# Three orders changed in a two-layer decoder trunk: half 1's first product, the turn of keys and probabilities, VectorE's work in the gating layer

## The chip, the core and the metric

One core of a Trainium2 chip runs the whole program. The metric is device microseconds of one execution, the median of several runs. The engines named here are TensorE (PE; its weight loads are shown apart as PEld), VectorE (DVE), ScalarE (ACT), GpSimd (POOL) and SyncE (SP), which issues nearly all loads. Work on different engines is ordered by semaphores alone.

## The reference

x is (1, 256, 1024) in float32. Two layers follow each other, each of four sub-layers:

```python
def reference(x, p, ...):
    for i in range(DEPTH):                      # DEPTH = 2
        x = layer_norm(DN_ALPHA * x + 0.5 * swiglu(x, w_gate, w_up, w_down), ...)
        m = mixer_attention(x, ...) if i % 2 == 0 else mixer_sgu(x, ...)
        x = layer_norm(DN_ALPHA * x + m, ...)
        x = layer_norm(DN_ALPHA * x + 0.5 * swiglu(x, ...), ...)
        x = x + jax.nn.sigmoid(x @ ple_w_gate[i]) * (p[i] @ ple_w_proj[i])

def mixer_sgu(x, w_in, b_in, ln_g, ln_b, w_s, b_s, w_out):
    u, v = jnp.split(jax.nn.gelu(x @ w_in + b_in), 2, axis=-1)
    v = layer_norm(v, ln_g, ln_b).reshape(...)
    mixed = jnp.einsum('gts,bcsgd->bctgd', jnp.where(causal, w_s, 0), v) + b_s...
    return (u * mixed) @ w_out
```

mixer_attention projects x to queries, keys and values of two groups of 8 heads (head size 64), runs softmax attention with a relative bias in the first group and with a forgetting term in the second, and projects the result back. The feed-forward width is 2816.

## The kernel before

The 256 tokens are two halves of 128, h = 0 and 1. Eight phases follow each other (`PHASES`): feed-forward, attention, feed-forward, gated embedding, and the same with the gating layer (`sgu`) in place of attention.

**Products in two parts.** Each float32 operand is split into a high part (ScalarE's copy into fp32r) and a low part (VectorE's subtraction, L1118). A product is high x high, high x low and low x high, three matmuls for each block of 128 input channels (L388, L389, L390). The stationary operand is the transposed x (xT_hi, xT_lo), the moving one the weights (g_hi, g_lo), 512 columns at a time. One gate product (`g_product`) is 8 blocks x 3 = 24 matmuls in two parts: part 0 takes blocks 0 to 3, whose weights come through rawA, part 1 blocks 4 to 7, through rawB.

**Weights.** SP loads a half of a chunk (two DMAs of 512 KB) into rawA or rawB, ScalarE copies it to g_hi, VectorE subtracts it to g_lo. g_hi and g_lo have two slots. The load of half n into a raw buffer waits for `split_a` or `split_b`, that is until VectorE has subtracted half n - 1 of that same buffer (`load_half`). A product of half 0 waits for the same semaphores before each of its parts.

**Borders between phases.** x is normalised half by half, turned by TensorE into the tp banks (L466, four 128x128 transposes for each of two blocks j), copied high by ScalarE (signal `tp_hi[j]`) and low by VectorE (signal `tp_taken[j]`). `g_product_turning` makes half 0's first product of a phase and puts half 1's transposes in front of and behind its last block. Half 1's first product follows; `x_wait` makes it wait for `tp_taken`, so for both parts of x, before each of its parts.

**Attention.** The order of the phase is written out in `ATTN_ORDER`, which TensorE, ScalarE and VectorE all walk. `("turn", c, h)` turns projected queries or keys from stage into tp bank h, `("probs", n)` turns head n's probabilities into bank n % 2, `("values", n)` multiplies heads 2n and 2n+1 with the values, and `("g front", 5, 0)` and `("g back", 5, 0)` are the two parts of a gate product. ScalarE's copy of probabilities n into probsT (L830) also waits until the values of head n - 2 are done with probsT. VectorE copies the turned keys to kT (L1383).

**Gating layer.** Eight products (four chunks, two halves) are followed by the output projection, chunks g0+4 and g0+5, in the order of `PAIR`: first chunk half 0, second chunk half 0, first chunk half 1, second chunk half 1. Before them VectorE makes y = gate times u of each half (`gate_y`, L1514, eight instructions), which TensorE turns (`y_turn`) and ScalarE and VectorE split into xT_hi and xT_lo. `biased` (L1505) adds the bias to a product and frees its bank; `lo_g(n, part)` is the subtraction of weight half `part` of chunk n. `y_turn(1)` stands between the two parts of the second of the four products.

Of the kernel before, what the change touches and what calls it, by code (L numbers as in the profile page):

```python
# [62 lines left out]
    ("g", 3, 1), ("probs", 0), ("probs", 1), ("scores", 1), ("exps", 1), ("turn", 3, 0), ("values", 0),  # L63
    ("g", 4, 0), ("probs", 2), ("probs", 3), ("scores", 2), ("exps", 2), ("turn", 3, 1), ("values", 1),
    ("g", 4, 1), ("probs", 4), ("probs", 5), ("scores", 3), ("exps", 3), ("turn", 4, 0),
    ("g front", 5, 0), ("probs", 6), ("probs", 7), ("values", 2), ("turn", 4, 1), ("g back", 5, 0), ("causal", 4),
    ("values", 3), ("scores", 4), ("exps", 4), ("group out", 0), ("causal", 5),
    ("g front", 5, 1), ("probs", 8), ("probs", 9), ("g back", 5, 1), ("scores", 5), ("exps", 5), ("causal", 6),
    ("proj", 0), ("p_copy", 0), ("w_out", 0), ("values", 4), ("w_low", 0), ("proj", 1), ("w_out", 1), ("p_copy", 1),
# [35 lines left out]
def p_use(k, c, h):  # L105


    return 1 if k == P_PHASE and c >= 2 - h else 0
# [24 lines left out]
def build(nc, bucket_onehot, x_in, p_in, ln_g, ln_b, w_gate, w_up, w_down, attn_w_in, attn_b_f, attn_w_out,  # L133
# [15 lines left out]
    with ExitStack() as ctx:  # L149
# [234 lines left out]
        def _(pe):  # L384
# [8 lines left out]
            def g_piece(slot, h, dst, k_from, k_to):  # L393
# [4 lines left out]
                               [g_hi[:, slot, b, :] for b in ks], [g_lo[:, slot, b, :] for b in ks],  # L398
                               first=k_from == 0, last=k_to == KB)

            def g_product(n, slot, h, dst, operand_wait=None, between=None, parts=(0, 1), front=None):
                for part in parts:
                    if operand_wait is not None:
                        operand_wait(part, h)
                    if h == 0:
                        pe.wait_ge((split_a, split_b)[part], n)
                    done = g_piece(slot, h, dst, 4 * part, 4 * part + 4)
                    if part == 0 and front is not None:
                        done.then_inc(front, 1)
                    if part == 0 and between is not None:  # L410
                        between()
                done.then_inc(g_done, 1)
# [101 lines left out]
            for k, (kind, i, s) in enumerate(PHASES):  # L514
# [4 lines left out]
                if kind == "ffn":  # L519
                    def up(c, cs, h, between=None, operand_wait=None):  # L520
                        bank_free(h, u0 + c)
                        g_product(g0 + c, (g0 + cs) % 2, h, gu[h][:, :], operand_wait, between)

                    def turn(c, cs, h):
                        pe.wait_ge(gu_taken[h], u0 + c + 1)
                        transposes(h, t0 + c + p_use(k, cs, h), [stage[:, h, FC + P * b:FC + P * b + P] for b in range(2)])

                    def down(c, cs, h, js=(0, 1)):

                        pe.wait_ge(tp_taken[h], t0 + c + (2 if k == P_PHASE and cs >= 1 else 1))  # L530
                        if k == 0 and cs == 0 and h == 1:
                            pe.wait_ge(bias_sb, 1)
                        at = 2 if h == 1 and cs == NCH - 1 else h
                        d_product(d0 + c, (d0 + cs) % 2, h, hT_hi[:, at], hT_lo[:, at], first=cs == 0,
                                  last=cs == NCH - 1, js=js)

                    def chunk(c, cs):

                        up(c, cs, 0)
                        turn(c - 1, cs - 1, 1)  # L540
                        down(c - 1, cs - 1, 0)
                        up(c, cs, 1)
                        turn(c, cs, 0)
                        down(c - 1, cs - 1, 1)

                    if k == 0:
                        g_first(x_wait)
                    elif PHASES[k - 1][0] == "ple":
                        up(0, 0, 0, half1, x_wait)
                    else:  # L550
                        bank_free(0, u0)
                        g_product_turning(g0, g0 % 2, 0, gu[0][:, :], x_wait, half1_block)
                    if k > 0:
                        up(0, 0, 1, operand_wait=x_wait)
                    if k == 0:
                        pe.wait_ge(bias_in, 32)
                        pe.matmul(acc[1][0:HEADS, 1, :], rel_sb[:, :], onehot_sb, start=True,
                                  stop=True).then_inc(bias_mm, 1)
                    turn(0, 0, 0)
                    chunk(1, 1)  # L560
                    if k == P_PHASE:
                        pe.wait_ge(p_loaded, 16 * (i + 1))
                        for h in range(HALVES):

                            transposes(h, t0 + 2 - h, [p_tok[:, h, P * b:P * b + P] for b in range(2)])
                    with pe.Fori(0, (NCH - 3) // 2) as r:
                        for e in range(2):
                            chunk(r * 2 + (2 + e), 2 + e)


                    c = NCH - 1
                    up(c, c, 0)
                    turn(c - 1, c - 1, 1)
                    down(c - 1, c - 1, 0)
                    turn(c, c, 0)
                    bank_free(1, u0 + c)
                    g_piece((g0 + c) % 2, 1, gu[1][:, :], 0, 2)
                    down(c, c, 0)
                    g_piece((g0 + c) % 2, 1, gu[1][:, :], 2, KB).then_inc(g_done, 1)
                    down(c - 1, c - 1, 1, (0,))  # L580
                    turn(c, c, 1)
                    down(c - 1, c - 1, 1, (1,))
                    use = (t0 + NCH + p_use(k, c, 0), t0 + NCH + p_use(k, c, 1) + 1)
                    ln_turn(0, x0, use)
                    down(c, c, 1)

                    def half1(x0=x0, use=use):
                        ln_turn(1, x0, use)

                    def half1_block(j, x0=x0, use=use):  # L590
                        ln_turn_block(1, j, x0, use)
# [40 lines left out]
                if kind == "attn":  # L632
# [62 lines left out]
                    for e in ATTN_ORDER:  # L695
                        if e[0] == "g":
                            c, h = e[1:]
                            bank_free(h, u0 + c)
                            if c == 0 and h == 0:
                                g_product_turning(g0, g0 % 2, 0, gu[0][:, :], x_wait, half1_block)  # L700
                            else:
                                g_product(g0 + c, (g0 + c) % 2, h, gu[h][:, :], x_wait if c == 0 else None)
                        elif e[0] == "g front":
                            c, h = e[1:]
                            bank_free(h, u0 + c)
# [61 lines left out]
                if kind == "sgu":  # L767
                    def mix(h):

                        pe.wait_ge(vn_ready, 2 * (h + 1))  # L770
                        for g in range(HEADS):
                            done = pe.matmul(acc[h][:, g // 4, P * (g % 4):P * (g % 4) + P], ws_T[:, g, :],
                                             v_sgu[:, h, P * g:P * g + P], start=True, stop=True)
                        done.then_inc(mix_done, 1)

                    def y_turn(h):
                        token_transposes(t_tok, h, t0 + h, [(tok_ready, x0 + 2 * h + j + 1) for j in range(2)])


                    for n, (c, h) in enumerate((c, h) for c in range(4) for h in range(2)):  # L780
                        bank_free(n % 2, u0 + n // 2)
                        if n == 0:
                            g_product_turning(g0 + c, (g0 + c) % 2, h, gu[0][:, :], x_wait, half1_block)
                        else:
                            g_product(g0 + c, (g0 + c) % 2, h, gu[n % 2][:, :], x_wait if c == 0 else None)
                        if n == 0:

                            pe.wait_ge(ws_loaded, 1)
                            for g in range(HEADS):
                                done = pe.transpose(acc[0][:, g // 4, P * (g % 4):P * (g % 4) + P],  # L790
                                                    ws_tok[:, g, :], ident[:, :])
                            done.then_inc(ws_turned, 1)
                        if n == 5:
                            pe.wait_ge(ws_taken, 1)
                            mix(0)
                        if n == 7:
                            y_turn(0)
                            mix(1)
                    use, out0, after = (t0, t0 + 1), g0 + 4, (t0 + 2, t0 + 3)

                    def y_wait(j, h, use=use):
                        pe.wait_ge(tp_taken[j], use[h] + 1)


                if kind in ("attn", "sgu"):
                    for n, (j, h) in enumerate(PAIR):
# [8 lines left out]
                        if n == 3 and kind == "sgu":  # L815
# [2 lines left out]
                                  y_wait if n % 2 == 0 else None, between,  # L818
                                  (1,) if j == 0 and kind == "attn" else (0, 1),
                                  out_front_done if n == 2 and kind == "sgu" else None)  # L820
                    use = after

                    def half1_block(j, x0=x0 + 4, use=use):
                        ln_turn_block(1, j, x0, use)
# [283 lines left out]
        def _(dve):  # L1108
# [19 lines left out]
            def lo_g(n, part):  # L1128
                lo_g_into(n, n % 2, part)
# [103 lines left out]
            for k, (kind, i, s) in enumerate(PHASES):  # L1233
# [264 lines left out]
                if kind == "sgu":  # L1498
# [41 lines left out]
                    biased(6, 3)  # L1540
                    lo_g(g0 + 4, 0)
                    gate_y(0)
                    lo_g(g0 + 4, 1)
                    xT_low(0, v0)
                    biased(7, 3)
                    gate_y(1)
                    for part in range(2):
                        lo_g(g0 + 5, part)
                    residual(0, 0, r0, (g_done, 2 * (g0 + 4) + 1))
                    xT_low(1, v0)  # L1550
                    ln0, out0, end = ln0 + 1, g0 + 4, v0 + 2
# [136 lines left out]
```

## Time and profile before

| | us |
|---|---|
| median of three runs | 1023.72 |
| lowest and highest | 1022.42, 1024.78 |
| the profiled execution | 1023.21 |
| its span | 1021.7 |

| engine | busy us | share of the span |
|---|---|---|
| PE | 1012.8 | 99% |
| PEld | 836.2 | 82% |
| DVE | 610.1 | 60% |
| ACT | 448.5 | 44% |
| POOL | 41.9 | 4% |

The span is the time from the first to the last recorded instruction. A matmul's end is modelled, so TensorE's share says that it is nearly always issued to, not that it runs at its peak. Where a wait matters, the distance between the starts of two instructions is the safer measure.

### The profile page before, as it was taken

What the parts mean: (1) busy time and instruction counts of PE and PEld (TensorE: products, weight loads), DVE (VectorE), ACT (ScalarE), POOL (GpSimd) and SP (SyncE); (2) the same over time, 40 slices, a digit from 0 to 9 for tenths busy, and PEclk for the clock granted to TensorE, in tenths of its full rate; (3) what the DMA queues carried; (4) which work ended last, traced back from release to release, by engine and by line L of the source; (5) the groups of instructions that cost most, each with busy time, mean ns of one, the idle gap of its engine ahead of it and who ended that gap; (6) DMA issues with size and microseconds to landing.
All of it is one profiled execution on the core that took longest, in us unless ns stands there. A gap on an engine that the chain in (4) does not pass through costs nothing.

```text
span 1021.7 us, 12789 instructions
## 1 busy us (share of the span) xinstructions
PE 1012.8 (99%) x4816; PEld 836.2 (82%) x4816; DVE 610.1 (60%) x716; ACT 448.5 (44%) x523; POOL 41.9 (4%) x55
## 2 busy tenths in 40 slices
PE   9999999999999999999999999999999999999998
PEld 7888888888888888888888888888887888888887
DVE  5655455776478745454677544545778864545574
ACT  5444344346473643434356343434344553434441
POOL 0400000100000000000010000000210100000010
PEclk9999999999999999999999999999999999999999
DMA  8875656355236766565539656564467676465531
GB/s 289 283 230 177 208 171 210 114 178 172 83 110 220 250 204 205 164 205 164 165 128 321 210 165 206 165 212 156 135 194 238 204 250 206 164 207 171 196 124 42
DMA packets 129683, 191.47 MB, mean 187 GB/s; under 512 B 5448, under 2 KB 95816, under 8 KB 129520
## 3 DMA queue, kind: packets, MB, share of 16 engines
q1 hardware_dynamic: 126432, 180.11, 53.9%
q0 software_dynamic: 2928, 10.61, 3.1%
q8 instruction: 24, 0.39, 0.2%
q10 hardware_dynamic: 288, 0.26, 0.1%
q14 instruction: 11, 0.09, 0.0%
HBM read 189.90 MB, written 1.06 MB: 187 GB/s over the span
## 4 chain that ended last, share of the span: by engine, by line
PE 93%; DVE 4%; DMA 1%; ACT 1%; issue 1%; SPq 0%; DVEq 0%; ACTq 0%
PE gu L388 19%; PE gu L390 19%; PE gu L389 19%; PE acc L388 10%; PE acc L390 10%; PE acc L389 10%; PE tp L466 4%; DVE g_lo L1118 2%; DMA rawB<-in_sgu_w_in 1%; ACT g_hi L830 1%; PE acc L653 1%; DVE t_tok L1514 0%; DVE xT_lo L1118 0%; DMA x_tok<-in_x 0%; DVE stage L1505 0%
## 5 line engine op out<-in xcount | busy, mean ns | idle before, releaser
L388 PE MATMUL gu<-g_hi,xT_hi 128*128 128x512 f32 x928 | 363.5, 392 | 1.2 <-DVE xT_lo L1118 1.1
L390 PE MATMUL gu<-g_hi,xT_lo 128*128 128x512 f32 x928 | 361.0, 389 | 0.0
L389 PE MATMUL gu<-g_lo,xT_hi 128*128 128x512 f32 x928 | 360.4, 388 | 0.0
L388 PEld LDWEIGHTS gu<-g_hi,xT_hi 128*128 128x128 f32 x928 | 174.3, 188 | 37.5 <-issue 2.4
L390 PEld LDWEIGHTS gu<-g_hi,xT_lo 128*128 128x128 f32 x928 | 174.2, 188 | 36.2
L389 PEld LDWEIGHTS gu<-g_lo,xT_hi 128*128 128x128 f32 x928 | 174.3, 188 | 34.8
L896 ACT ACTIVATE stage<-gu 128x256 f32<-128x256 f32 x88 | 33.7, 383 | 361.2 <-PE gu L390 361.1
L1118 DVE TENSOR_TENSOR g_lo<-rawA,g_hi 128x2048 fp32r<-128x2048 f32 (+2 forms) x66 | 141.5, 2145 | 78.4 <-ACT g_hi L830 78.3
L1118 DVE TENSOR_TENSOR g_lo<-rawB,g_hi 128x2048 fp32r<-128x2048 f32 (+1 forms) x64 | 141.0, 2203 | 18.1 <-ACT g_hi L830 18.1
L1244 DVE SCALAR_TENSOR_TENSOR stage<-stage,gu 128x256 f32<-128x256 f32 x88 | 37.0, 420 | 189.6 <-ACT stage L896 189.6
L388 PE MATMUL acc<-d_hi,hT_hi 128*128 128x512 f32 x352 | 144.8, 411 | 0.0
L830 ACT ACTIVATE g_hi<-rawA 128x2048 fp32r<-128x2048 f32 (+2 forms) x66 | 118.6, 1800 | 46.4 <-DMA rawA<-in_ffn_w_up 26.0
L390 PE MATMUL acc<-d_hi,hT_lo 128*128 128x512 f32 x352 | 138.1, 392 | 0.0
L389 PE MATMUL acc<-d_lo,hT_hi 128*128 128x512 f32 x352 | 137.6, 391 | 0.0
L1118 DVE TENSOR_TENSOR d_lo<-rawD,d_hi 128x2048 fp32r<-128x2048 f32 x45 | 103.1, 2292 | 46.0 <-ACT d_hi L830 46.0
L830 ACT ACTIVATE g_hi<-rawB 128x2048 fp32r<-128x2048 f32 (+1 forms) x64 | 118.3, 1849 | 17.5 <-DMA rawB<-in_ffn_w_up 6.9
L830 ACT ACTIVATE d_hi<-rawD 128x2048 fp32r<-128x2048 f32 x45 | 86.4, 1920 | 6.3 <-DMA rawD<-in_ffn_w_down 4.2
L390 PEld LDWEIGHTS acc<-d_hi,hT_lo 128*128 128x128 f32 x352 | 66.0, 188 | 14.6
L389 PEld LDWEIGHTS acc<-d_lo,hT_hi 128*128 128x128 f32 x352 | 66.5, 189 | 11.6
L388 PEld LDWEIGHTS acc<-d_hi,hT_hi 128*128 128x128 f32 x352 | 66.1, 188 | 11.2
L1626 POOL TENSOR_TENSOR small<-small 128x1 f32<-128x1 f32 x14 | 18.0, 1288 | 879.5 <-DVE small L1155 879.5
L1118 DVE TENSOR_TENSOR hT_lo<-tp,hT_hi 128x256 fp32r<-128x256 f32 x88 | 36.9, 419 | 9.8 <-ACT hT_hi L830 9.8
(181 smaller groups left out, 673.1 us busy)
## 6 DMA issues: line engine op xcount, KB each, us to landing
rawD<-in_ffn_w_down SPq DMA_DIRECT2D x44, 1024.0 KB, 4.9
rawA<-in_ffn_w_gate SPq DMA_DIRECT2D x42, 512.0 KB, 4.0
rawA<-in_ffn_w_up SPq DMA_DIRECT2D x42, 512.0 KB, 4.9
rawB<-in_ffn_w_gate SPq DMA_DIRECT2D x42, 512.0 KB, 4.4
rawB<-in_ffn_w_up SPq DMA_DIRECT2D x42, 512.0 KB, 5.5
rawA<-in_attn_w_in SPq DMA_DIRECT2D x12, 512.0 KB, 4.4
rawB<-in_attn_w_in SPq DMA_DIRECT2D x12, 512.0 KB, 4.9
rawA<-in_ple_w_gate SPq DMA_DIRECT2D x8, 512.0 KB, 4.7
```

Source lines behind the costliest of these rows:

```text
L388: pe.matmul(dst, hi[b], w_hi[b], start=first and b == 0, stop=False)
L389: pe.matmul(dst, hi[b], w_lo[b], start=False, stop=False)
L390: done = pe.matmul(dst, lo[b], w_hi[b], start=False, stop=last and b == len(hi) - 1)
L466: done = pe.transpose(tp[bank][0:src.shape[1], rows * q:rows * q + rows], src, ident[0:rows, 0:rows])
L653: done = pe.matmul(acc[0][:, r, at:at + P], qT[rows, blk, i_q * P:i_q * P + P], kT[rows, blk, keys:keys + P], start=g == 0, stop=g == 0 or ...
L830: return act.activation(dst, src, ACT.Copy, scale=scale)
L896: act.activation(stage[:, h, 0:FC], gu[h][:, 0:FC], ACT.Silu).then_inc(act_done, 1)
L1118: return dve.tensor_tensor(dst, src, hi.bitcast(F32), ALU.subtract)
L1244: dve.scalar_tensor_tensor(out=stage[:, h, FC:2 * FC], in0=stage[:, h, 0:FC], scalar=0.5, in1=gu[h][:, FC:2 * FC], op0=ALU.mult, op1=ALU.m ...
L1626: pool.tensor_tensor(rstd[:, h:h + 1], var_eps[:, h:h + 1], neg_half, ALU.pow)\
```

## The change

Three edits, in one.

1. Half 1's first product of a phase, at the four borders that `g_product_turning` serves, becomes `g_product_high_first`. It waits for `tp_hi[0]` first, makes the eight matmuls of blocks 0 to 3 that take x's high part, then waits for x's low part and makes the four low x high ones. Part 1 is as before.
2. In `ATTN_ORDER` the keys of the second group, half 1, are turned ahead of the values of heads 4 and 5 and of the probabilities of heads 6 and 7.
3. In the gating layer VectorE makes x's low part and the last bias add ahead of weight half B of chunk g0+4, and weight half A of chunk g0+5 ahead of `gate_y(1)`.

```diff
-    ("g front", 5, 0), ("probs", 6), ("probs", 7), ("values", 2), ("turn", 4, 1), ("g back", 5, 0), ("causal", 4),
+    ("g front", 5, 0), ("turn", 4, 1), ("values", 2), ("probs", 6), ("probs", 7), ("g back", 5, 0), ("causal", 4),
...
+            def g_product_high_first(slot, dst, high_use, operand_wait):
+
+                tok = slice(P, 2 * P)
+                pe.wait_ge(tp_hi[0], high_use)
+                for b in range(4):
+                    pe.matmul(dst, xT_hi[:, b, tok], g_hi[:, slot, b, :], start=b == 0, stop=False)
+                    pe.matmul(dst, xT_hi[:, b, tok], g_lo[:, slot, b, :], start=False, stop=False)
+                operand_wait(0, 1)
+                for b in range(4):
+                    pe.matmul(dst, xT_lo[:, b, tok], g_hi[:, slot, b, :], start=False, stop=False)
+                operand_wait(1, 1)
+                g_piece(slot, 1, dst, 4, KB).then_inc(g_done, 1)
...
-                    if k > 0:
+                    if k > 0 and PHASES[k - 1][0] == "ple":
                         up(0, 0, 1, operand_wait=x_wait)
+                    elif k > 0:
+                        bank_free(1, u0)
+                        g_product_high_first(g0 % 2, gu[1][:, :], high_use, x_wait)
...
                     biased(6, 3)
                     lo_g(g0 + 4, 0)
                     gate_y(0)
-                    lo_g(g0 + 4, 1)
                     xT_low(0, v0)
                     biased(7, 3)
+                    lo_g(g0 + 4, 1)
+                    lo_g(g0 + 5, 0)
                     gate_y(1)
-                    for part in range(2):
-                        lo_g(g0 + 5, part)
+                    lo_g(g0 + 5, 1)
                     residual(0, 0, r0, (g_done, 2 * (g0 + 4) + 1))
```

TensorE at the border from the first feed-forward phase to attention, start of half 1's first product; before:

```order
L388 MATMUL gu<-g_hi,xT_hi 128x512 [waits tp_taken0,gu_taken1]
L389 MATMUL gu<-g_lo,xT_hi 128x512
L390 MATMUL gu<-g_hi,xT_lo 128x512
L388 MATMUL gu<-g_hi,xT_hi 128x512
L389 MATMUL gu<-g_lo,xT_hi 128x512
```

and now:

```order
L406 MATMUL gu<-g_hi,xT_hi 128x512 [waits tp_hi0,gu_taken1]
L407 MATMUL gu<-g_lo,xT_hi 128x512
L406 MATMUL gu<-g_hi,xT_hi 128x512
L407 MATMUL gu<-g_lo,xT_hi 128x512
L406 MATMUL gu<-g_hi,xT_hi 128x512
L407 MATMUL gu<-g_lo,xT_hi 128x512
L406 MATMUL gu<-g_hi,xT_hi 128x512
L407 MATMUL gu<-g_lo,xT_hi 128x512
L410 MATMUL gu<-g_hi,xT_lo 128x512 [waits tp_taken0]
L410 MATMUL gu<-g_hi,xT_lo 128x512 x3
L388 MATMUL gu<-g_hi,xT_hi 128x512 [waits tp_taken1]
```

The low-x matmul moved from third place to ninth, and the wait for VectorE's part (tp_taken0) with it.

VectorE in the gating layer, from the gating of half 0 on (t_tok from acc and u_sgu is `gate_y`, stage from gu is `biased`); before:

```order
L1514 SCALAR_TENSOR_TENSOR t_tok<-acc,small,u_sgu 128x128 x7
L1118 TENSOR_TENSOR g_lo<-rawB,g_hi 128x2048 [waits high_b]
L1118 TENSOR_TENSOR xT_lo<-tp,xT_hi 128x4x128 [waits tp_hi0]
L1118 TENSOR_TENSOR xT_lo<-tp,xT_hi 128x4x128 [waits tp_hi1]
L1505 TENSOR_TENSOR stage<-gu,bias_tab 128x512 [waits act_done,g_done]
L1514 SCALAR_TENSOR_TENSOR t_tok<-acc,small,u_sgu 128x128 [waits act_done,mix_done]
L1514 SCALAR_TENSOR_TENSOR t_tok<-acc,small,u_sgu 128x128 x7
L1118 TENSOR_TENSOR g_lo<-rawA,g_hi 128x2048 [waits high_a]
L1118 TENSOR_TENSOR g_lo<-rawB,g_hi 128x2048 [waits high_b]
```

and now:

```order
L1535 SCALAR_TENSOR_TENSOR t_tok<-acc,small,u_sgu 128x128 x7
L1139 TENSOR_TENSOR xT_lo<-tp,xT_hi 128x4x128 [waits tp_hi0]
L1139 TENSOR_TENSOR xT_lo<-tp,xT_hi 128x4x128 [waits tp_hi1]
L1526 TENSOR_TENSOR stage<-gu,bias_tab 128x512 [waits act_done,g_done]
L1139 TENSOR_TENSOR g_lo<-rawB,g_hi 128x2048 [waits high_b]
L1139 TENSOR_TENSOR g_lo<-rawA,g_hi 128x2048 [waits high_a]
L1535 SCALAR_TENSOR_TENSOR t_tok<-acc,small,u_sgu 128x128 [waits act_done,mix_done]
L1535 SCALAR_TENSOR_TENSOR t_tok<-acc,small,u_sgu 128x128 x7
L1139 TENSOR_TENSOR g_lo<-rawB,g_hi 128x2048 [waits high_b]
```

The first g_lo from rawB moved behind x's low part and the bias add, and the g_lo from rawA ahead of the gating of half 1. The last row, the second chunk's half B, kept its place as the last of these. The number of instructions on both engines is the same, and the orders of ScalarE, SP and POOL are unchanged.

## Rows read from the trace of the kernel before

**Rows 1.** Page: busy times; granted TensorE clock in 40 slices.

```profile
PE 1012.8 (99%) x4816; PEld 836.2 (82%) x4816; DVE 610.1 (60%) x716; ACT 448.5 (44%) x523; POOL 41.9 (4%) x55
...
PEclk9999999999999999999999999999999999999999
```

**Rows 2.** Waits of TensorE, whole span: us in total, times, longest.

```profile
PE gu L388 <- DVE xT_lo L1118: 1.1, 3, 0.4
...
PE acc L388 <- DVE g_lo L1118: 0.6, 1, 0.6
```

**Rows 3.** Timeline, border into attention: start, duration (us), instruction, [idle before <-releaser].

```profile
201.04 0.60 PE L466 MATMUL tp<-ident,x_tok 128*128 128x128 f32 x4
...
201.40 0.48 PE L388 MATMUL gu<-g_hi,xT_hi 128*128 128x512 f32 x1
...
201.68 0.60 ACT L830 ACTIVATE xT_hi<-tp 128x512 fp32r<-128x512 f32 x1 [5.34 <-PE tp L466]
...
202.18 0.60 PE L466 MATMUL tp<-ident,x_tok 128*128 128x128 f32 x4
202.31 0.69 DVE L1118 TENSOR_TENSOR xT_lo<-tp,xT_hi 128x512 fp32r<-128x512 f32 x1 [1.24 <-ACT xT_hi L830]
...
203.14 0.47 PE L388 MATMUL gu<-g_hi,xT_hi 128*128 128x512 f32 x1 [0.37 <-DVE xT_lo L1118]
```

**Rows 4.** Timeline, attention around the turn of the second group's keys.

```profile
266.09 0.60 ACT L830 ACTIVATE stage<-gu 128x512 f32<-128x512 f32 x1 [2.92 <-PE gu L390]
...
270.78 0.81 PE L466 MATMUL tp<-ident,probs 128*128 128x128 f32 x6
...
272.98 0.49 ACT L830 ACTIVATE probsT<-tp 128x384 f32<-128x384 f32 x1 [0.18 <-PE acc L676]
...
273.58 0.42 PEld L466 LDWEIGHTS tp<-ident,stage 128*128 128x128 f32 x4 [0.84 <-issue]
```

**Rows 5.** Timeline, gating layer's output projection, TensorE.

```profile
776.66 0.19 PEld L388 LDWEIGHTS acc<-g_hi,xT_hi 128*128 128x128 f32 x1 [0.55 <-DVE xT_lo L1118]
...
782.99 0.50 PE L388 MATMUL acc<-g_hi,xT_hi 128*128 128x512 f32 x1 [0.60 <-DVE g_lo L1118]
...
785.84 1.03 PE L466 MATMUL tp<-ident,t_tok 128*128 128x128 f32 x8
...
786.63 0.48 PE L388 MATMUL acc<-g_hi,xT_hi 128*128 128x512 f32 x1
```

**Rows 6.** The same stretch, VectorE, ScalarE and SP.

```profile
773.72 2.28 DVE L1118 TENSOR_TENSOR g_lo<-rawB,g_hi 128x2048 fp32r<-128x2048 f32 x1
...
773.96 1.20 ACT L830 ACTIVATE xT_hi<-tp 128x512 fp32r<-128x512 f32 x2 [2.22 <-PE tp L466]
...
775.92 1.28 DVE L1118 TENSOR_TENSOR xT_lo<-tp,xT_hi 128x512 fp32r<-128x512 f32 x2
776.03 0.88 SPq L317 DMA_DIRECT2D rawB<-in_sgu_w_out  x2
...
777.12 0.68 DVE L1505 TENSOR_TENSOR stage<-gu,bias_tab 128x512 f32<-128x512 f32 x1
...
778.57 2.16 DVE L1514 SCALAR_TENSOR_TENSOR t_tok<-acc,small,u_sgu 128x128 f32<-128x128 f32 x8 [0.77 <-ACT u_sgu L1063]
...
782.20 1.91 ACT L830 ACTIVATE g_hi<-rawB 128x2048 fp32r<-128x2048 f32 x1 [1.92 <-DMA rawB<-in_sgu_w_out]
...
784.14 2.29 DVE L1118 TENSOR_TENSOR g_lo<-rawB,g_hi 128x2048 fp32r<-128x2048 f32 x1 [1.21 <-ACT g_hi L830]
```

**Rows 7.** Issue to landing: tile rawA, 771 to 784 us; tile rawB, 760 to 790.

```profile
DMA to landing us min/median/max: 4.1/4.7/5.3
...
DMA to landing us min/median/max: 3.8/4.8/5.7
```

**Rows 8.** Timeline, start of the program, TensorE.

```profile
1.60 2.93 PE L506 MATMUL acc<-ident 128*128 128x128 f32 x12 [1.60 <-POOL ident L1575]
...
4.76 1.12 PE L466 MATMUL tp<-ident,x_tok 128*128 128x128 f32 x4 [0.23 <-DMA x_tok<-in_x]
```

More of the change, by code:

```diff
@@ L583, in _ @@
                     use = (t0 + NCH + p_use(k, c, 0), t0 + NCH + p_use(k, c, 1) + 1)
+                    high_use = B["v"] + NCH + p_use(k, c, 0) + 2
                     ln_turn(0, x0, use)
@@ L700, in _ @@
                                 g_product_turning(g0, g0 % 2, 0, gu[0][:, :], x_wait, half1_block)
+                            elif c == 0:
+                                g_product_high_first(g0 % 2, gu[1][:, :], high_use, x_wait)
                             else:
-                                g_product(g0 + c, (g0 + c) % 2, h, gu[h][:, :], x_wait if c == 0 else None)
+                                g_product(g0 + c, (g0 + c) % 2, h, gu[h][:, :])
                         elif e[0] == "g front":
@@ L783, in _ @@
                             g_product_turning(g0 + c, (g0 + c) % 2, h, gu[0][:, :], x_wait, half1_block)
+                        elif n == 1:
+                            g_product_high_first(g0 % 2, gu[1][:, :], high_use, x_wait)
                         else:
-                            g_product(g0 + c, (g0 + c) % 2, h, gu[n % 2][:, :], x_wait if c == 0 else None)
+                            g_product(g0 + c, (g0 + c) % 2, h, gu[n % 2][:, :])
                         if n == 0:
@@ L820, in _ @@
                                   out_front_done if n == 2 and kind == "sgu" else None)
-                    use = after
+                    use, high_use = after, B["v"] + 4
                     def half1_block(j, x0=x0 + 4, use=use):
```

## The prediction

> **What bounds the kernel now.** I read the page first. TensorE is busy 1012.8 of 1021.7 us and the granted clock stays in its top tenth in all 40 slices [rows 1], so the time is TensorE's issue plus its few waits: an edit can give back only a wait, or make a new one. The view of waits, cut to TensorE, came next. Three first matmuls of a gate product wait for the low part of x, 1.1 us together, and one matmul into acc waits 0.6 for the low part of a weight half [rows 2]. These figures start from a modelled end of the matmul before, so I took the sizes from the timelines, from start to start.
>
> **Half 1's first product.** It follows the two transposes of half 1 at four phase borders. At the first, four transposes start at 201.04 and the next matmul at 201.40, 0.36 later: that is the pitch without a wait. The second four start at 202.18, so the product could start at 202.54; it starts at 203.14 [rows 3]. The wait is 0.60 us. It is for the VectorE subtraction (202.31 to 203.00). Now the first eight matmuls need only ScalarE's copy, which runs from 201.68 to 202.28 [rows 3], 0.26 before 202.54. Eight matmuls, each at least 1012.8 / 4816 = 0.21 us [rows 1], then cover the low part: it is usable at 203.05 and wanted at 204.2. The second block's low part comes about 1.1 later, against a need at 205.1. The number of matmuls and weight loads is the same. Only three of the four borders wait [rows 2]: before the gating layer, eight transposes of ws_tok stand between, and nothing goes there. 3 x 0.60 = 1.8 us saved. The bound below is the view's own 1.1.
>
> I looked at what is late next behind each. The weight halves of chunk 1 in the feed-forward and attention phases are converted before they are wanted by more than 0.6, and DMA, ScalarE and VectorE there start from TensorE's own signals, so an earlier TensorE draws them along. I take nothing off for that.
>
> **Keys turned ahead of probabilities.** Probabilities are transposed at 270.78; the value products need ScalarE's earlier copies; then the key transposes want the second tp bank, which is free only once ScalarE has copied the new probabilities out of it (from 272.98, held until the value products release probsT). TensorE's weight load sat idle 0.84 before 273.58 [rows 4]. In the new order the keys go first. Their source was in place long before (copied to stage from 266.09 for 0.60), and the bank was left by the copies of the former pair. Value products (1.3 us) then cover VectorE's copy of the keys (0.7) out of that bank before the probabilities want it. The probabilities' copies start some 0.7 later on ScalarE, and so does its next g_hi copy; the back half of the product, 12 matmuls or 2.85 us, lies over them. Saved: 0.84, and 0 to 0.84 as bounds, because the 0.7 us of lag on ScalarE might be met again later in the phase. I take 0.8.
>
> **Gating layer, VectorE's order.** Before: low part of weight half B of the first output chunk (773.72 to 776.00), low part of x (775.92, two blocks, 1.28), bias add (777.12), gating of half 1 (778.57 to 780.73), low part of half A of the second chunk, then half B (784.14) [rows 6]. TensorE waits twice: its weight load 0.55 before 776.66, and then at 782.99, when the 24 matmuls from 776.66, at 2.85 or a little less for twelve (782.99 to 785.84), were used up near 782.3, so some 0.7 [rows 5].
>
> After: x's low part follows ScalarE's copy (from 773.96, two of 0.60 [rows 6]), so 774.6 to 775.9; bias add to 776.5; half B of the first chunk from 776.40 to 778.68. TensorE can start at 776.66 - 0.55 = 776.11 and wants that half B twelve matmuls on, at 778.95: just met. Half A of the second chunk waits for its ScalarE copy. Its rawA was issued at 771.8 to 772.2 and lands by 5.3 after [rows 7], 777.5; copied by 779.5, subtracted by 781.8. TensorE wants it at 781.7 and starts the second product near 781.85, 1.15 ahead of before. That is what the edit pays.
>
> What it costs stands in SP's row. The second chunk's half B is reloaded into rawB only when the first chunk's half B has been subtracted: the issue at 776.03 is 0.03 behind 776.00 [rows 6]. That subtraction now ends at 778.68, 2.7 later, so the issue moves to 778.71. Before, this chain had nothing to spare: rawB landed and ScalarE started at 782.20 after waiting 1.92 for it, VectorE ended at 786.43 after waiting 1.21 for ScalarE, and the matmul that needs it started at 786.63, 0.79 behind the transposes at 785.84 [rows 5, 6]. From ScalarE's start to the low part being usable is 4.28. From issue to ScalarE's start it was 6.17. A load of rawB here lands 3.8 to 5.7 after its issue, 4.8 in the middle [rows 7], and the second of the pair is issued 0.4 late: 5.2 in the middle, 6.1 at the end. Now nothing else is on its way, so I take 5.6: 778.71 + 5.6 + 4.28 = 788.6 against 786.63. That is 2.0 us later, bounds 1.6 (5.2) and 2.5 (6.1); with the quickest landing (4.2 in all) it would be 0.6. TensorE arrives there at 785.5 (1.15 early, half 1's gating being done by 783.9) and stands 3.1 us. The gain of 1.15 is inside this wait and counts for nothing.
>
> What follows (n = 2 and 3, the last chunk's loads, the next phase) hangs on TensorE and on this subtraction and moves with them.
>
> **Sum.** -1.8 - 0.8 + 2.0 = -0.6 us. The profiled execution took 1023.21 (span 1021.7 and 1.5 around it), which gives 1022.6; the median of the three runs, 1023.72, gives 1023.1. I say 1022.8. The bounds of the terms give -2.1 (2.64 saved, 0.6 lost) to +1.4 (1.1 saved, 2.5 lost).
>
> **Rivals.** (1) The clock falls in the new stand of 3.1 us. Against it: the granted clock stays in its top tenth (the 2.4 GHz level) all through [rows 1]; but the longest stand after the start is 0.84 [rows 4], so no row tests it. A price can be read at the start, where the same instructions run at half pace although the clock row does not show it: 12 matmuls in 2.93 from 1.60, four transposes 1.12 where later ones take 0.60 [rows 3, 8]. Twelve at the later pitch of 0.11 need 1.3, so 1.6 + 0.5 us, about 2.1, were lost there. Placed behind 788.6 it gives 1022.8 + 2.1 = 1024.9, 1.2 slower than the median before. It turns the sum to slower once it costs more than the 0.6 us of the forecast, some three matmuls at half pace. Chance 0.15.
> By the Trainium skill (TensorE: Matmul & The Clock Gate, "Why this matters for your kernels"), TensorE is to be kept from long idle gaps between bursts of matmuls, since they send it back to half rate. By that rule the 3.1 us stand could be such a gap, at the price just read; no trace so far shows whether it is.
> (2) The reload is hidden: rawB would have to land before 781 for TensorE's arrival at 785.5 to find the half ready. Then -1.8 - 0.8 - 1.15 = -3.8, 1019.5. Against it: 2.3 us after issue, where no row is under 3.8 [rows 7]. Chance 0.07.
> (3) The savings are not there: the copies still bind, or the attention and feed-forward loops give the 2.6 back later, while the gating layer's loss stays. 1022.8 + 2.6 = 1025.4. For it: the lag put on ScalarE behind the keys' turn, and loads paced by VectorE; against it: both loops start again from TensorE's own signals at each chunk. Chance 0.08.
> (4) Forecast as worked out, 0.62; the rest, 0.08, is mishaps of either sign.
>
> **How the numbers follow.** 0.2% (2.05 us) is about what a measurement of this kernel can tell from no change. The forecast lies inside it on nearly all its spread; rival 1 mostly too (+1.2), rival 3 half. Faster: rival 2 and the forecast's lower tail, 0.12. Slower: half of rival 3, a fifth of rival 1 and some mishaps, 0.10. Same: 0.78. The range runs from 1021.0 (the best of the terms, less the scatter of a median) to 1025.3 (rivals 1 and most of 3).
>
> **What would show it.** Right: no wait ahead of half 1's first product, its low-x matmuls in a block of four; no wait ahead of the key transposes; in the gating layer x's low part near 1.3 us earlier, SP's rawB issue 2.7 later, and TensorE standing some 3 us, released by g_lo from rawB, between the transposes of t_tok and the second half of the second product. Wrong: a stand there under 1 us (rival 2), a clock below 1.00 or matmul spacings near 0.45 just behind it (rival 1), or TensorE waits over 0.3 in attention or behind a border that were not there (rival 3).

## The result, and the profile after

| | before | after |
|---|---|---|
| median of 22 runs each, us | 1022.82 | 1024.52 |
| lowest and highest | 1022.16, 1024.78 | 1022.66, 1026.94 |
| profiled execution, span | 1023.21, 1021.7 | 1024.58, 1023.0 |

The ratio is 1.0016, 95% interval 1.0011 to 1.0022: the change costs 1.7 us (1.1 to 2.3). The forecast was 1022.8, 0.6 under its own starting point. The result is inside the range, but on the other side of no change.

From the page of the kernel after, the rows that answer to [rows 1]:

```profile
PE 1013.1 (99%) x4816; PEld 837.4 (82%) x4816; DVE 610.4 (60%) x716; ACT 448.1 (44%) x523; POOL 41.9 (4%) x55
...
PE   9999999999999999999999999999998999999998
...
PEclk9999999999999999999999999999999999999999
```

Little shows here: one slice of this page is some 25 us, and what happened lasts 6.5. The row of the clock is unchanged; TensorE's own row has one 8 (767 to 793 us) where the kernel before has a 9. The view of waits, cut to TensorE, says more (us in total, times, longest):

```profile
PE acc L388 <- DVE g_lo L1139: 2.8, 1, 2.8
...
PE tp L479 <- DVE hT_lo L1139: 1.4, 1, 1.4
```

The three waits for x's low part of [rows 2] are gone. The one for the low part of a weight half, 0.6 before, is now 2.8, as was forecast, and one has come that was not: 1.4 ahead of the transposes of p_tok near 831 us.

**The border into attention**, timeline of TensorE, against [rows 3]:

```profile
201.96 0.60 PE L479 MATMUL tp<-ident,x_tok 128*128 128x128 f32 x4
202.31 0.48 PE L406 MATMUL gu<-g_hi,xT_hi 128*128 128x512 f32 x1
...
204.24 1.07 PE L410 MATMUL gu<-g_hi,xT_lo 128*128 128x512 f32 x4
```

0.35 from the second transposes to the product, where it was 0.96: 0.61 saved. At the other two borders the same distances are 0.35 and 0.36, where they were 0.97.

**The keys' turn**, against [rows 4]:

```profile
269.95 0.60 PE L479 MATMUL tp<-ident,stage 128*128 128x128 f32 x4
270.38 0.33 PE L690 MATMUL acc<-v_att,probsT 128*128 128x64 f32 x2
...
271.67 0.82 PE L479 MATMUL tp<-ident,probs 128*128 128x128 f32 x6
272.25 0.47 PE L388 MATMUL gu<-g_hi,xT_hi 128*128 128x512 f32 x1
```

Keys, values, probabilities and the back half of the product follow each other without a stand. That back half starts 1.75 earlier than before (274.00), of which 0.9 belongs to this edit; the rest is the border's 0.61 and 0.2 that this execution was ahead at 201 us.

**The gating layer's output projection**, TensorE, against [rows 5]:

```profile
770.48 1.17 PE L479 MATMUL tp<-ident,t_tok 128*128 128x128 f32 x8
773.19 0.47 PE L388 MATMUL acc<-g_hi,xT_hi 128*128 128x512 f32 x1
...
781.57 1.03 PE L479 MATMUL tp<-ident,t_tok 128*128 128x128 f32 x8
785.38 0.72 PE L388 MATMUL acc<-g_hi,xT_hi 128*128 128x512 f32 x1 [2.78 <-DVE g_lo L1139]
785.90 0.63 PE L389 MATMUL acc<-g_lo,xT_hi 128*128 128x512 f32 x1
786.33 0.63 PE L390 MATMUL acc<-g_hi,xT_lo 128*128 128x512 f32 x1
...
788.46 0.60 PE L389 MATMUL acc<-g_lo,xT_hi 128*128 128x512 f32 x1
788.89 0.41 PE L390 MATMUL acc<-g_hi,xT_lo 128*128 128x512 f32 x1
789.13 0.39 PE L388 MATMUL acc<-g_hi,xT_hi 128*128 128x512 f32 x1
...
795.30 1.04 PE L479 MATMUL tp<-ident,x_tok 128*128 128x128 f32 x8
```

The rows of before that [rows 5] doesn't have, for the distances below:

```profile
773.32 1.20 PE L466 MATMUL tp<-ident,t_tok 128*128 128x128 f32 x8
...
788.54 0.39 PE L390 MATMUL acc<-g_hi,xT_lo 128*128 128x512 f32 x1
...
794.90 1.04 PE L466 MATMUL tp<-ident,x_tok 128*128 128x128 f32 x8
```

Read the first column of the kernel after. The transposes of 781.57 end their issue 0.8 later, and the next product starts at 785.38: TensorE stands 3.0 us. Then come eight slow matmuls (0.52 from the first to the second, 0.43 from start to start after that), and from 788.89 on they come at 0.23 again. VectorE, ScalarE and SP of the same stretch, against [rows 6]:

```profile
771.75 1.29 DVE L1139 TENSOR_TENSOR xT_lo<-tp,xT_hi 128x512 fp32r<-128x512 f32 x2 [0.81 <-ACT xT_hi L851]
...
773.55 2.28 DVE L1139 TENSOR_TENSOR g_lo<-rawB,g_hi 128x2048 fp32r<-128x2048 f32 x1
...
775.86 0.89 SPq L317 DMA_DIRECT2D rawB<-in_sgu_w_out  x2
...
781.09 1.91 ACT L851 ACTIVATE g_hi<-rawB 128x2048 fp32r<-128x2048 f32 x1 [4.75 <-DMA rawB<-in_sgu_w_out]
...
783.03 2.29 DVE L1139 TENSOR_TENSOR g_lo<-rawB,g_hi 128x2048 fp32r<-128x2048 f32 x1 [2.30 <-ACT g_hi L851]
```

SP's reload of rawB is issued 5.38 us behind the transposes of t_tok (770.48); before it was 2.71 (776.03 less 773.32). The windows of TensorE's clock (window, length, busy and count of PE, PEld, DVE, ACT, POOL, granted clock, DMA share, GB/s):

```profile
780.00:785.00 5.00, 2.60 (x16) 2.04 (x14) 2.70 (x4) 2.88 (x3) 0.00 (x0) 1.00 0.72 243
785.00:790.00 5.00, 4.62 (x13) 3.67 (x14) 2.80 (x5) 0.00 (x0) 0.00 (x0) 0.66 0.68 207
790.00:795.00 5.00, 5.00 (x23) 4.12 (x23) 4.61 (x9) 1.92 (x1) 0.99 (x1) 1.00 0.01 2
```

The granted clock is 0.66 as a mean over the window that holds the end of the stand and the slow matmuls: part of it at 1.2 GHz, the rest at 2.4. Eight matmuls took 3.51 us (785.38 to 788.89); before, the same eight took 1.91 (786.63 to 788.54). In this execution the clock costs 1.6 us.

### The profile page after: what moved, and what is told of

The parts are those of the page before. It is cut to its first block, busy times and chain, and to the rows that moved or that the text cites. A ratio compares the mean times of both kernels' runs of the same rounds, so it can differ in the third digit from the quotient of the medians.

```text
span 1023.0 us, 12789 instructions
## 1 busy us (share of the span) xinstructions
PE 1013.1 (99%) x4816; PEld 837.4 (82%) x4816; DVE 610.4 (60%) x716; ACT 448.1 (44%) x523; POOL 41.9 (4%) x55
## 4 chain that ended last, share of the span: by engine, by line
PE 94%; DMA 2%; DVE 2%; ACT 1%; issue 0%; SPq 0%; POOL 0%; ACTq 0%
PE gu L388 20%; PE gu L390 20%; PE gu L389 20%; PE acc L388 9%; PE acc L389 9%; PE acc L390 9%; PE tp L479 4%; DVE g_lo L1139 1%; DMA rawB<-in_ffn_w_up 1%; PE acc L670 1%; DMA ws_tok<-in_sgu_w_s 0%; DMA rawB<-in_sgu_w_out 0%; ACT g_hi L851 0%; DMA x_tok<-in_x 0%; PE gu L406 0%; PE gu L407 0%
## 5 line engine op out<-in xcount | busy, mean ns | idle before, releaser
L388 PE MATMUL gu<-g_hi,xT_hi 128*128 128x512 f32 x912 | 357.0, 391 | 0.0
L390 PE MATMUL gu<-g_hi,xT_lo 128*128 128x512 f32 x912 | 354.8, 389 | 0.0
L389 PE MATMUL gu<-g_lo,xT_hi 128*128 128x512 f32 x912 | 354.2, 388 | 0.0
L390 PEld LDWEIGHTS gu<-g_hi,xT_lo 128*128 128x128 f32 x912 | 171.2, 188 | 35.6
L388 PEld LDWEIGHTS gu<-g_hi,xT_hi 128*128 128x128 f32 x912 | 171.3, 188 | 35.2 <-issue 0.6
L389 PEld LDWEIGHTS gu<-g_lo,xT_hi 128*128 128x128 f32 x912 | 171.4, 188 | 34.3
```

What stands on the lines that cost most here:

```text
L388: pe.matmul(dst, hi[b], w_hi[b], start=first and b == 0, stop=False)
L389: pe.matmul(dst, hi[b], w_lo[b], start=False, stop=False)
L390: done = pe.matmul(dst, lo[b], w_hi[b], start=False, stop=last and b == len(hi) - 1)
```

## Experiments

Eleven runs follow, one of them the kernel before again. The median of the kernel before in the same batch is given beside a time. A length that recurs below is the **output stretch**: from the transposes of t_tok near 771 us to the eight transposes of x_tok near 795. Read inside one execution, it is free of what came before it. In the seven profiles that have the gating layer's old order it is 21.4 to 22.0.

### The two orders without VectorE's

```diff
                     gate_y(0)
+                    lo_g(g0 + 4, 1)
                     xT_low(0, v0)
                     biased(7, 3)
-                    lo_g(g0 + 4, 1)
-                    lo_g(g0 + 5, 0)
                     gate_y(1)
-                    lo_g(g0 + 5, 1)
+                    for part in range(2):
+                        lo_g(g0 + 5, part)
```

> The changed kernel with the gating layer's VectorE order put back to that of before; the other two edits stay. Reload theory: no stand between the transposes of t_tok and the second part of the second output product, no matmuls at 0.43 spacing, and the savings stay: three borders at 0.61 and the keys' turn at 0.84 or a little more, so 2.4 to 2.8 us under before. Rival (the savings are given back in the feed-forward loop, where TensorE stood 1.4 us at 830 us in the changed kernel for hT_lo): a stand of 1 us or more there and only 0.8 to 1.4 us under before.

1021.46 (11 runs), before 1023.19 (33): ratio 0.9983 [0.9974, 0.9992]. Half 1's product and the keys' turn are worth 1.7 us together (0.8 to 2.7), and the harm of the change is in the third edit. The stand and the slow matmuls are gone, and the output stretch is 21.76 us (771.35 to 793.11), as before. The 2.4 to 2.8 expected did not come: the rival's stand is there too, 1.3 us ahead of p_tok's transposes (829.89). It is taken up below.

### VectorE's order alone

The kernel before with the third edit of the change and nothing else.

> The kernel before with the gating layer's VectorE order of the change and nothing else. Reload theory with the clock: second part of the second output product 1.6 to 2.0 us later than before, then eight matmuls at 0.43 for 0.23 (1.65 more), so 3.2 to 3.7 us over before. Without the clock's part (rival: the half pace was chance in the one profile) 1.6 to 2.0 over. If the gating order is harmless and the rest of the change to blame: within 0.5 of before.

1025.9 (11 runs, same batch): ratio 1.0025 [1.0016, 1.0034], 2.6 us slower. That lies between the two answers expected, 3.2 to 3.7 with the clock and 1.6 to 2.0 without it; the filled kernels below say why. Its timeline has the stand and, behind its fourth matmul, the slow ones:

```profile
783.69 1.03 PE L466 MATMUL tp<-ident,t_tok 128*128 128x128 f32 x8
787.51 0.50 PE L388 MATMUL acc<-g_hi,xT_hi 128*128 128x512 f32 x1 [2.78 <-DVE g_lo L1118]
...
788.55 0.59 PE L389 MATMUL acc<-g_lo,xT_hi 128*128 128x512 f32 x1
788.94 0.63 PE L390 MATMUL acc<-g_hi,xT_lo 128*128 128x512 f32 x1
789.37 0.63 PE L388 MATMUL acc<-g_hi,xT_hi 128*128 128x512 f32 x1
```

The output stretch is 24.89 (772.53 to 797.42); in the kernel after it is 24.82 (770.48 to 795.30), in the kernel before 21.58 (773.32 to 794.90). So it is about 3.2 longer, whether the other edits are there or not: 1.6 to 1.7 because the weights come later, 1.6 from the slow matmuls.

### TensorE kept at work in the stand

The kernel after, with 12 matmuls of 512 columns behind the transposes, into a bank that is free; their result is not used.

```diff
-                            between = lambda: y_turn(1)
+                            def between():
+                                y_turn(1)
+                                pe.wait_ge(gu_taken[0], u0 + 4)
+                                for _ in range(12):
+                                    pe.matmul(gu[0][:, :], xT_hi[:, 0, 0:P], g_hi[:, out0 % 2, 0, :],
+                                              start=True, stop=True)
```

> The changed kernel with twelve more matmuls of 512 columns between the transposes of t_tok and the second part of the second output product, into gu's first bank, which is free then; their result is used by nothing. They fill 2.8 of the 3.0 us in which TensorE stands. Clock theory: the matmuls behind keep 0.23 spacing, 1.6 to 1.7 us under the changed kernel, though TensorE does more. Rival (slow matmuls come from something else, such as VectorE and DMA traffic at that place): still 0.43 behind the fill and no gain. In neither does the reload's own 1.6 us go.

1023.28 (11 runs, same batch as the two above): ratio 1.0004 [0.9995, 1.0013], where the change has 1.0016 [1.0011, 1.0022]. That is 1.2 us less by the ratios, for 1.6 to 1.7 expected, and the two intervals just touch, so the trace has to carry this. Timeline of TensorE, then the window behind the stand:

```profile
781.79 1.04 PE L479 MATMUL tp<-ident,t_tok 128*128 128x128 f32 x8
782.59 2.97 PE L837 MATMUL gu<-g_hi,xT_hi 128*128 128x512 f32 x12
785.54 0.50 PE L388 MATMUL acc<-g_hi,xT_hi 128*128 128x512 f32 x1
785.88 0.40 PE L389 MATMUL acc<-g_lo,xT_hi 128*128 128x512 f32 x1
```

```profile
785.00:790.00 5.00, 5.00 (x23) 3.83 (x22) 4.34 (x7) 0.00 (x0) 0.00 (x0) 1.00 0.64 201
```

The product starts no earlier against t_tok's transposes (14.81 us behind them, 14.90 in the kernel after), since its weights come no earlier, but the matmuls behind it keep their 0.23 and the clock its 1.00. The output stretch is 23.11 (770.73 to 793.84): 1.7 shorter than in the kernel after, and 1.5 longer than before. Work that nobody uses made this stretch shorter.

### The same filling on VectorE's order alone

> VectorE's order in the gating layer alone, on the kernel before, with 12 matmuls whose result is not used put into TensorE's stand of 2.8 us. If that order costs 2.7 us because of 1.2 us that the late reload adds and 1.5 us of half-pace matmuls behind the stand, this one is about 1.5 us under the order alone: 1024.4, ratio 1.0010, with no half-pace matmuls near 788 us and a granted clock of 1.00. If the whole loss were the late reload, it would be 1025.9, ratio 1.0025, as without the filling matmuls.

1025.25 (11 runs, before 1022.89 in 27; one execution of 5.9 ms left out): ratio 1.0022 [1.0012, 1.0031]. The size that was expected, 1024.4 or a ratio of 1.0010, did not come: it lies outside the interval, and the rival's 1.0025 inside. Against the order alone the medians, which come from two chips, show 0.7 of the 1.5 expected, the ratios 0.3. The trace does show what was expected of it:

```profile
784.22 1.03 PE L466 MATMUL tp<-ident,t_tok 128*128 128x128 f32 x8
785.00 2.98 PE L816 MATMUL gu<-g_hi,xT_hi 128*128 128x512 f32 x12
788.12 0.50 PE L388 MATMUL acc<-g_hi,xT_hi 128*128 128x512 f32 x1
...
796.46 1.04 PE L466 MATMUL tp<-ident,x_tok 128*128 128x128 f32 x8
```

No slow matmuls, and an output stretch of 23.36 (773.10 to 796.46), 1.5 under the order alone. It is still 1.8 over the kernel before, where the expectation had put 1.2 on the late reload.

One reason why the times show less is that the clock does not fall in every execution. Half pace for 3.5 of 1023 us takes 0.0017 off the mean clock of an execution, so 0.998 or less speaks for a fall and 0.999 or more against it. Of the 22 timed runs of the kernel after, 18 have 0.998 or less, with a median of 1024.66; the other four took 1022.66 to 1024.03. Of the 11 of VectorE's order alone, seven have 0.998, with a median of 1026.21; the other four have 1025.26, and the filled kernel 1025.25. All 21 filled runs (the one of 5.9 ms left out) have 0.999 or more. So the filling brings a kernel to where its executions without a fall are, or a little under. Why the clock falls in some executions and not in others was not tested.

### The reload made early

The kernel after, with the second output chunk's half B loaded into rawD, which is idle there, instead of rawB; it then needs only ScalarE's copy of the first chunk's half B to be made, not VectorE's subtraction.

```diff
+        spare_n = bases[5]["g"] + 5
+        raw_spare = rawD[:, :, :].rearrange("p c (b n) -> p (c b) n", n=512)
...
+                elif isinstance(n, int) and n == spare_n and part == 1:
+                    raw = raw_spare
+                    sp.wait_ge(split_d, bases[5]["d"])
+                    sp.wait_ge(high_b, n - 1)
```

> The changed kernel, but the second output chunk's half B is loaded into rawD, which is idle in the gating layer, as soon as ScalarE has copied the first chunk's half B, so its load no longer waits for VectorE's subtraction. Reload theory: it lands near 778 us instead of 783, VectorE subtracts it right behind the gating of half 1, TensorE waits under 1 us and the clock stays: 3.2 to 3.7 us under the changed kernel plus 0.5, so 1018.8 to 1020.3 us. Rival (VectorE's own sequence is the bound there, not the load): the stand stays above 2 us.

1021.32 (11 runs, same batch): ratio 0.9982 [0.9973, 0.9991]. SP's queue, ScalarE's copy, and TensorE behind its transposes at 781.37:

```profile
769.78 0.92 SPq L323 DMA_DIRECT2D rawD<-in_sgu_w_out  x2
```

```profile
777.99 1.92 ACT L857 ACTIVATE g_hi<-rawD 128x2048 fp32r<-128x2048 f32 x1 [2.02 <-DMA rawD<-in_sgu_w_out]
```

```profile
782.61 0.50 PE L394 MATMUL acc<-g_hi,xT_hi 128*128 128x512 f32 x1 [0.20 <-DVE g_lo L1147]
```

The load goes out 0.5 ahead of t_tok's transposes instead of 5.4 behind them, the stand is under 0.5 (0.2 by the view), the matmuls keep their 0.23, and the output stretch is 20.70 (770.23 to 790.93), 0.7 to 1.3 under the seven with the old order. So the reload was the cause of the stand, and in this stretch VectorE's order has a gain once the load is early. The timed runs don't show that gain: 1021.32, against 1021.46 for the kernel with the old order in the same batch, and over the 1018.8 to 1020.3 that was expected.

### The kernel before once more, and half 1's product alone

> The kernel before, unchanged, for a second profile. In five profiles of variants rawB's load for chunk 2 of the third feed-forward phase started ScalarE's copy 8.7 to 9.0 us after its issue, in the first profile of before 7.4. Theory (that first profile was a lucky one, the stand is there in before too): copy 8.7 to 9.0 after issue, and TensorE stands 0.8 to 1.1 us ahead of p_tok's transposes for hT_lo. Rival (the savings of the change make the stand): no stand, as in the first profile.

> The kernel before with half 1's first product by high x first, and nothing else. Theory with the stand in the third feed-forward phase: three borders give 0.61 each, the last one's is waited away before p_tok's transposes, so 1.2 us under before. Rival (nothing is given back): 1.8 under.

The kernel before, profiled again (1024.12, span 1022.6), has a stand that its first profile did not have. ScalarE's copy of the weights in the first profile, then the copy and TensorE in the second:

```profile
825.25 1.92 ACT L830 ACTIVATE g_hi<-rawB 128x2048 fp32r<-128x2048 f32 x1 [1.08 <-DMA rawB<-in_ffn_w_up]
```

```profile
826.59 1.92 ACT L830 ACTIVATE g_hi<-rawB 128x2048 fp32r<-128x2048 f32 x1 [2.45 <-DMA rawB<-in_ffn_w_up]
...
831.64 0.63 PE L466 MATMUL tp<-ident,p_tok 128*128 128x128 f32 x4 [0.77 <-DVE hT_lo L1118]
```

SP's load of rawB was issued at 817.78 and ScalarE could copy it 8.8 us later; in the first profile it was 7.4 (817.88 to 825.25), and in no other kernel with this order of work under 8.7. VectorE's subtraction of the weights then stands ahead of the hidden rows that TensorE wants.

Half 1's product alone: 1022.3 (11 runs, before 1023.28 in 16): ratio 0.9988 [0.9979, 0.9997], 1.2 us saved where three borders give 1.8. The interval (0.3 to 2.1) holds both answers, so this rests on the timeline at the same place, TensorE:

```profile
830.09 0.63 PE L479 MATMUL tp<-ident,p_tok 128*128 128x128 f32 x4 [1.41 <-DVE hT_lo L1139]
```

From the border's last transposes of x_tok (805.49) to this row it is 24.60, and in the kernel before, profiled again, 24.58 (807.06 to 831.64). The border is 0.61 shorter and the stand 0.64 longer: against an execution that has the stand, the third border's saving is waited away. The load of rawB is issued 10.7 behind those transposes in both (816.22; 817.78). SP issues it behind that of rawD, which waits for VectorE's subtraction of the half before, so VectorE's work paces it, not TensorE's product.

### The keys' turn alone

One line of `ATTN_ORDER`, as in the change.

> The kernel before with the keys' turn alone. Theory: its 0.84 us is earned at 273 us and nothing later gives it back, since every later load starts from TensorE's own signals and so moves with it; only what is saved inside the feed-forward chunk of the last stand (p_tok, near 831 us) or just ahead of it is waited away there. The ratio then is 0.9992 (0.8 under before) and the stand near 831 us keeps its 0.8 to 1.0 us. Rival: attention gives it back by ScalarE's lag of 0.7 us, ratio 1.0000, with a wait of 0.3 us or more on TensorE between 274 and 334 us that the kernel before does not have.

1022.04 (11 runs, before 1022.89 in 27): ratio 0.9989 [0.9980, 0.9998], 0.85 to 1.1 saved. The rival's 1.0000 is outside, though by little. From the end of the product's front half to the start of its back half it is 2.30 (270.50 to 272.80), where it was 3.22 (270.78 to 274.00): 0.92 in the trace. The stand near 831 has 0.81, about as in the second profile of before (0.77): this saving was made 500 us earlier, and the loads moved with it.

### The stand near 831 taken away

In chunk 1 of the third feed-forward phase ScalarE and VectorE make the gated rows and their transposed parts ahead of weight half B, not behind it (the edit for ScalarE; VectorE's is the same with `lo_g_into`):

```diff
-                        hi_g_into(c + (g0 + 1), slot, 1)
+                        turn_first = k == P_PHASE and cs == 1
+                        if not turn_first:
+                            hi_g_into(c + (g0 + 1), slot, 1)
...
+                        if turn_first:
+                            hi_g_into(c + (g0 + 1), slot, 1)
```

On the first experiment's kernel:

> High x first and keys first, gating layer as before, and in chunk 1 of the third feed-forward phase ScalarE and VectorE make the gate and the low part of hT ahead of weight half B. Theory: the stand of 1.3 us before p_tok's transposes goes, 1.2 to 1.5 us under the run without it (so 3.0 to 3.3 under before), and the whole 0.61 of the last border is kept. Rival (the late load binds elsewhere): a new wait at the gate product of chunk 3 that takes it back, within 0.3 of the run without.

1019.88 (5 runs, before 1023.28 in 16): ratio 0.9965 [0.9951, 0.9979], 3.4 under before for 3.0 to 3.3 expected. The stand is gone, and from x_tok's last transposes (804.45) to this row it is 23.03:

```profile
827.48 0.60 PE L479 MATMUL tp<-ident,p_tok 128*128 128x128 f32 x4
```

On the kernel before:

> The kernel before with one edit that the change does not have: in chunk 1 of the third feed-forward phase ScalarE and VectorE make the gate and the transposed hidden rows ahead of weight half B. If the stand before the p_tok transposes (0.8 to 1.0 us in the kernel before) is the rule and the first profile without it the exception, the ratio is 0.9991 (0.9 under before) and the stand is gone. If the stand is rare in the kernel before and only the changed kernels have it, the ratio is 1.0000.

1022.5 (11 runs, before 1022.89 in 27): ratio 0.9995 [0.9986, 1.0004]. The stand is gone here too (23.65 from 807.07 to 830.72, which is 0.62 more than the 23.03 above, the border's saving now kept). The time moved by half of what was expected, and its interval holds both answers, so how often the kernel before stands there is not settled: two profiles, one with and one without.

### All of it

The kernel with rawD and that feed-forward order.

> The changed kernel with the second output chunk's half B in rawD and with that order of chunk 1 in the third feed-forward phase. If both causes are what they seem, no stand over 0.7 us is left: 1.2 to 1.5 under the run with rawD alone, 1019.6 to 1020.2, and 3.0 to 3.5 under before.

1019.87 (6 runs, before 1023.28 in 16): ratio 0.9967 [0.9955, 0.9979]. It beats the kernel before by 3.4 us, and by the ratios the kernel after by some 5, as expected. TensorE's waits after the start, all of them:

```profile
PE tp L485 <- DVE xT_lo L1151: 0.6, 1, 0.6
PE acc L394 <- DVE g_lo L1151: 0.3, 1, 0.3
```

It is not faster than the kernel without VectorE's order and with the feed-forward one (1019.88), although its span is 1.0 shorter in the profiles (1017.3, 1018.3). Five and six runs don't tell them apart.

## Why the prediction was wrong

**The step that failed is the choice in rival (1)**: whether the clock falls in the stand. The forecast had the stand (3.1 us; measured 3.0), put the clock's part in the sum at nothing, and gave the other way a chance of 0.15. It fell, and its 1.6 us turned a sum that was near nothing into a slower kernel. The filled stand shows that it was this: with the same wait and no idle TensorE the slow matmuls are gone. The price was read at the start of the program as 2.1 (12 matmuls and four transposes at half pace) and came out as 1.6, since eight matmuls ran slow. The mistake was in the weighing: no row of before had an idle stretch longer than 0.84 behind the start, so the trace could not speak against the fall, and the start itself, half pace after an idle stretch of 1.6 us, spoke for it. That the granted clock stayed in its top tenth all through said only that no such stand had been there.

The Trainium skill's rule (TensorE: Matmul & The Clock Gate, "Why this matters for your kernels"), that long idle gaps between bursts of matmuls send TensorE back to half rate, held here: clock 0.66 and starts 0.43 apart behind 3.0 idle us, and neither behind the 1.4 of the stand near 831. By the mean clock it held in 18 of 22 executions. By that rule the forecast would have been rival (1), 1024.9, a change of +1.5; the median is 1024.52 and the change +1.7. That it comes so near is in part luck: its price of the clock is 0.5 too high and its reload 0.4, against 0.6 saved that was not kept.

**The reload** was right in its chain and nearly in its size. Issue 2.7 later against t_tok's transposes: 2.67. From issue to ScalarE 5.6: 5.23. From ScalarE's start to the low part 4.28: 4.29. The wait's end moved by +1.6 (785.38 - 770.48 = 14.90, before 786.63 - 773.32 = 13.31) where I took 2.0; 1.6 was the lower of my two bounds. That the stand came out as forecast hides two errors of size: TensorE arrived 1.4 earlier (11.09 behind t_tok's transposes, before 12.52), not 1.15, and the weights came 0.4 less late.

**Half 1's product** was right at the borders, 0.61 for 0.60, and wrong behind the third: "I take nothing off for that" failed. There 0.6 is waited away near 831 us. I looked at the weights of chunk 1 alone; the wait comes from weight half B of chunk 2, which VectorE subtracts ahead of the hidden rows of chunk 1, and the one profile of before was an execution without it. This is rival (3) for a quarter of its 2.6.

**The keys' turn** was right: 0.8 taken, 0.92 in the trace, 0.85 to 1.1 in the time by itself, and the view of waits has nothing for TensorE between 274 us and the next border in the kernel after, so ScalarE's lag was not met.

**The starting point.** The three runs of before had a median of 1023.72, 22 have 1022.82. The forecast's 1022.8 lay between 1022.6 (from the profiled run) and 1023.1 (from that median); against 1022.82 the same sum says 1022.2.

Set together from what was measured: -1.2 (three borders less the one given back) - 0.9 + 1.6 + 1.6 = +1.1, against +1.7 [1.1, 2.3] in the runs. So the sum lies at the edge of the interval, and the 0.6 between them was not traced to a place. Two things in it are open: the clock's 1.6 is not paid in every execution, and the -1.2 takes it that the kernel before has the stand near 831, of which one profile has it and one has not.

## What to carry to other kernels

Ask of each new wait not only how long it is but whether TensorE stands idle through it: behind 3.0 idle us here came eight matmuls at half pace, 1.6 us on top. Where an edit moves the instruction that frees a load buffer, move the load first (a spare buffer took away the 2.6 us that the same order had cost, though no more than that in the timed runs). And profile the kernel before twice: a stand that depends on when a load lands can be missing from one execution, and it swallows what is saved just ahead of it.

## What the runs showed of the hardware

- The granted clock fell for about 3.5 us and left no mark in the clock row of a page with 25-us slices. The mean clock of an execution shows it as a rule (0.998 against 0.999 to 1.000), but not surely: one of the 33 runs of before beside the first four experiments reads 0.949 with an ordinary time (1023.50). The first slow matmul is not always the first behind the stand: in VectorE's order alone four came at 0.23 to 0.33 before eight at 0.39 to 0.43.
- At the program's start the half pace stands in the starts and not in the clock, which reads 1.00 in the window of 1.60 to 3.00 us too; behind the stand at 785 it stands in both.
- A pair of 512 KB loads into rawB reached ScalarE 5.2 us behind its issue at 776 us, with nothing issued in the 6 us ahead of it, and another such pair 7.4 to 9.0 us behind it near 818 us, with 1 MB for rawD issued 0.6 ahead of it. No run tests that this 1 MB is the reason.
